# Projection phases of a two-layer decoder: another order at their start, weights of k converted ahead of tile 0, the norm gain in the output weights

## The reference

```python
for l in range(DEPTH):
    mod = silu(c) @ ada_w[l] + ada_b[l]                 # 6 rows of 1024
    sh1, sc1, g1, sh2, sc2, g2 = split(mod, 6)
    h = x * (1 + sc1) + sh1
    y = mlstm_mixer(h) if l == 0 else dilated_mixer(h, k_sh, v_sh, w_q, w_o)
    x = layer_norm(ALPHA * x + (1 + g1) * y, ...)
    h = x * (1 + sc2) + sh2
    x = layer_norm(ALPHA * x + (1 + g2) * hier_moe(h), ...)
    if l == 0:
        kv = x @ b_w_kv                                 # k and v, 3 * 8 * 64 columns each
        k_sh, v_sh = rope(kv[k]), kv[v]

def mlstm_mixer(h):
    q, k, v, o_gate, gates = split(h @ w_in)
    ht = mlstm_chunkwise(q, k, v, gates)                # (heads, tokens, 256)
    hn = (ht - mean) * rsqrt(var + 1e-6) * norm_g       # norm_g: 1024 gains
    return (hn * sigmoid(o_gate)) @ w_out
```

## Time and profile before

| | us |
|---|---|
| runs before, median of 3 | 4450.17 (4449.74 to 4456.16) |
| the profiled execution | 4457.96 |
| its span in the trace | 4456.2 |
| PE busy | 3855.9 (87% of the span) |
| DVE busy | 2224.4 (50%) |
| ACT busy | 1409.7 (32%) |
| POOL busy | 536.3 (12%) |

### The profile page before, as it was taken

How to read it: one execution, slowest core, us unless ns; L and a number is a source line. 1 busy time by engine, 2 the same in 40 slices (tenths; PEclk the granted TensorE clock), 3 DMA queues, 4 the chain that set the end, 5 groups by cost and what they waited for, 6 DMA issues and landing times. The chain is left out here.

```text
span 4456.2 us, 54326 instructions
## 1 busy us (share of the span) xinstructions
PE 3855.9 (87%) x17420; PEld 2852.8 (64%) x17420; DVE 2224.4 (50%) x4969; ACT 1409.7 (32%) x2977; POOL 536.3 (12%) x469
## 2 busy tenths in 40 slices
PE   6999794979949999995996998989996949999990
PEld 4777574868735565554885776868885736556550
DVE  3222314865455555556763333225436845555557
ACT  2212202632213333332222113216565413333334
POOL 0100000110001111104540002321000001111103
PEclk8999896979959999997998998999997959999995
DMA  6433312643239999986645433225454339999988
GB/s 232 142 119 122 124 66 98 194 141 105 74 120 391 389 388 391 389 317 202 191 147 182 170 138 110 77 73 174 120 161 167 128 108 384 389 391 389 389 330 316
DMA packets 662249, 951.11 MB, mean 213 GB/s; under 512 B 42317, under 2 KB 532765, under 8 KB 640845
## 3 DMA queue, kind: packets, MB, share of 16 engines
q1 hardware_dynamic: 607118, 772.87, 50.6%
q0 software_dynamic: 27360, 99.63, 5.8%
q10 hardware_dynamic: 27632, 76.87, 4.4%
HBM read 746.62 MB, written 202.65 MB: 213 GB/s over the span
## 5 line engine op out<-in xcount | busy, mean ns | idle before, releaser
L1517 PE MATMUL ex_gu<-ex_wgu,ex_hT 128*128 128x512 f32 x2016 | 911.2, 595 | 11.6 <-DMA ex_wgu<-in_moe_w_up_dram 8.0
L1517 PEld LDWEIGHTS ex_gu<-ex_wgu,ex_hT 128*128 128x128 f32 x2016 | 375.4, 191 | 388.3 <-issue 378.3
L1644 DVE TENSOR_TENSOR ex_wds<-ex_wd,ex_wds 128x2048 fp32r<-128x2048 f32 x126 | 288.8, 2292 | 247.2 <-ACT ex_wds L1577 247.2
L1535 PE MATMUL ex_acc<-ex_wds,ex_aT 128*128 128x512 f32 x1512 | 384.9, 404 | 7.7 <-DVE ex_aT L1640 7.7
L2199 PE MATMUL pvo_mm<-pvo_ws,pvo_hT 128*128 128x512 f32 x1536 | 360.7, 395 | 19.8 <-POOL pvo_hT L2348 18.4
L2199 PEld LDWEIGHTS pvo_mm<-pvo_ws,pvo_hT 128*128 128x128 f32 x1536 | 288.8, 190 | 83.4 <-POOL pvo_hT L2348 19.2
L1535 PEld LDWEIGHTS ex_acc<-ex_wds,ex_aT 128*128 128x128 f32 x1512 | 277.8, 190 | 65.1 <-DVE ex_aT L1640 8.1
L992 PE MATMUL am_acc<-am_ws,am_yT 128*128 128x512 f32 x1152 | 296.4, 413 | 19.7 <-issue 15.2
L1592 ACT ACTIVATE ex_sg<-ex_gu 128x256 f32<-128x256 f32 x126 | 48.4, 384 | 834.5 <-PE ex_gu L1517 834.5
L2199 PE MATMUL pk_mm<-pk_ws,pk_hT 128*128 128x512 f32 x1152 | 274.7, 397 | 28.4 <-DVE pk_part L2336 16.9
L2199 PE MATMUL pq_mm<-pq_ws,pq_hT 128*128 128x512 f32 x1152 | 268.4, 394 | 20.0 <-POOL pq_hT L2348 20.0
(11 more groups left out here) (337 smaller groups left out, 5655.0 us busy)
## 6 DMA issues: line engine op xcount, KB each, us to landing
ex_wgu<-in_moe_w_gate_dram SPq DMA_DIRECT2D x126, 1024.0 KB, 9.0
ex_wgu<-in_moe_w_up_dram SPq DMA_DIRECT2D x126, 1024.0 KB, 12.3
ex_wd<-in_moe_w_down_dram SPq DMA_DIRECT2D x126, 1024.0 KB, 6.5
ybuf_scratch<-ex_y ACTq DMA_DIRECT2D x126, 512.0 KB, 6.7
pv_m_w<-in_ada_w_dram SPq DMA_DIRECT2D x16, 1536.0 KB
pvo_r_w<-in_ada_w_dram SPq DMA_DIRECT2D x32, 512.0 KB
vo_scratch<-pvo_vo SPq DMA_DIRECT2D x16, 1024.0 KB, 5.0
x_scratch<-am_x SPq DMA_DIRECT2D x32, 512.0 KB, 3.0
```

The source lines that it names most:

```text
L1517: ins = nc.tensor.matmul(gu[j][:, :, :], hT[:, j, k, :], wgu[:, jw, k, :, :], start=(k == 0), stop=(k == KD - 1))
L1535: ins = nc.tensor.matmul(acc[half][:, :], aT[:, hi_a, k, :], wds[:, j, hi_w, k, half * CH:(half + 1) * CH], start=(k == 0 and n == 0), sto ...
L1644: nc.vector.tensor_tensor(wds[:, j, 1, :, :], wd[:, j, :, :], wds[:, j, 0, :, :], ALU.subtract).then_inc(wlo_ready, 1)
```

## The change

- **Projections, start.** SP first loads tile 0 (in k: `dest`, then tile 0's rows) and the identity and columns; the other tables follow, then tile 1 and the weights. ACT and DVE begin with the weight pieces and wait for the columns and constants only behind them. `FIRST` becomes 4 in vo, all 12 in k, 2 in v and q. The memset of v's value buffer and the start of the woven modulation move behind all weights.
- **k.** `dest` has a semaphore of its own, the only one that POOL's gather waits for. There is no `rest_of_weights`; tile 0's transposed copy and split run one step earlier (lead 2) than those of the other tiles.
- **vo.** The store of tile 0's `full` is put among the weight loads, behind piece 8. RestOfModulation's stages run one tile earlier, with two PSUM banks in place of one, and its store comes last in SP's list.
- **v.** LaterModulation's total runs one tile later, and DVE makes the partial before it adds the previous tile's bias.
- **mlstm and after_mixer of layer 0.** `ng` and `norm_gain` go; `gate` multiplies the normalised rows by the output gate directly. `MixerWeights` loads the gain as 128 x 8 (4 KB); ACT scales by it in `weights_hi`, DVE in `weights_lo`, each in two operations of 128 x 512 per piece in place of one of 128 x 1024.

```diff
@@ mlstm
-                sp.dma_start(ng[:, :], d["a_norm_g"][0:1, :].to_broadcast([P, D])).then_inc(c_in, 16)
...
                 def divide(c, j):
                     act.wait_ge(rden_ready, c + 1)
-                    wait_from(act, ng_done, c - 1)
+                    wait_from(act, y_ready, c - 1)
...
                 def gate(c, j):
                     dve.wait_ge(og_in[j], 8 * (c - j) + 16)
-                    dve.wait_ge(ng_done, c + 1)
-                    nc.vector.tensor_tensor(y[:, j, :], y[:, j, :], og[:, j, :], ALU.mult).then_inc(y_ready, 1)
+                    wait_from(dve, stored[j], 8 * (c - j))
+                    dve.wait_ge(hn_ready, c + 1)
+                    nc.vector.tensor_tensor(y[:, j, :], ht[:, j, :, :].rearrange("p h e -> p (h e)"), og[:, j, :], ALU.mult).then_inc(y_ready, 1)
...
-                def norm_gain(c, j):
-                    pool.wait_ge(hn_ready, c + 1)
-                    wait_from(pool, stored[j], 8 * (c - j))
-                    nc.gpsimd.tensor_tensor(y[:, j, :], ht[:, j, :, :].rearrange("p h e -> p (h e)"), ng[:, :], ALU.mult).then_inc(ng_done, 1)
-
-                skewed(pool, [(norm_gain, -1)])
@@ MixerWeights.load
         sp.dma_start(self.gain[:, :], d["mod"][self.l:self.l + 1, 2 * D:3 * D].to_broadcast([P, D])).then_inc(self.gain_in, 16)
+        if self.l == 0:
+            sp.dma_start(self.ng[:, :], d["a_norm_g"][0].rearrange("(p k) -> p k", k=self.K)).then_inc(self.ng_in, 16)
@@ after_mixer, weights_hi and weights_lo
-                        nc.scalar.activation(ws[:, 0, rows, cut], w[:, rows, cut], ACT.Copy).then_inc(whi_ready, 1)
+                            nc.scalar.activation(ws[:, 0, rows.start, cut], w[:, rows.start, cut], ACT.Copy, scale=mw.ng[:, rows.start:rows.start + 1])
+                            rows = slice(rows.start + 1, rows.stop)
+                        nc.scalar.activation(ws[:, 0, rows, cut], w[:, rows, cut], ACT.Copy, scale=1.0 if l else mw.ng[:, rows]).then_inc(whi_ready, 1)
...
-                        v.tensor_tensor(ws[:, 1, rows, cut], w[:, rows, cut], ws[:, 0, rows, cut], ALU.subtract).then_inc(wlo_ready, 1)
+                            for k in range(rows.start, rows.stop):
+                                ins = v.scalar_tensor_tensor(ws[:, 1, k, cut], w[:, k, cut], mw.ng[:, k:k + 1], ws[:, 0, k, cut], ALU.mult, ALU.subtract)
+                            ins.then_inc(wlo_ready, 1)
@@ RestOfModulation
-        self.acc = ph.ps("r_acc", [P, CW])
+        self.acc = [ph.ps(f"r_acc{s}", [P, CW]) for s in range(2)]
-        return [(load, 0), (store, -1)]
+        return [(load, 1), (store, 0)]
...
-                wait_from(pe, self.row_ready, n)
-                self.nc.tensor.matmul(self.acc[0:1, :], self.ones[:, :], self.part[:, s, :], start=True, stop=True).then_inc(self.acc_ready, 1)
-        return [(total, -1)]
+                wait_from(pe, self.row_ready, n - 1)
+                self.nc.tensor.matmul(self.acc[s][0:1, :], self.ones[:, :], self.part[:, s, :], start=True, stop=True).then_inc(self.acc_ready, 1)
+        return [(total, 0)]
...
-        return [(add_bias, -1), (partial, 0)]
+        return [(add_bias, 0), (partial, 1)]
@@ LaterModulation
-        return [(total, 0)]
+        return [(total, -1)]
-        return [(add_bias, -1), (partial, 0)]
+        return [(partial, 0), (add_bias, -1)]
@@ Combine
+    def sync_dest(self, sp):
+        sp.dma_start(self.dest[:, :, :].rearrange("p c j -> p (c j)"), self.d["dest"]).then_inc(self.dest_in, 16)
@@ project
-        FIRST = KD // WK
+        FIRST = {"vo": KD // WK, "k": KD // WK * NBK, "v": 2, "q": 2}[which]
...
+        def first_tile(stage):
+            return lambda c, j: stage(c, j) if isinstance(c, int) and c == 0 else None
+        def later_tiles(stage):
+            return lambda c, j: None if isinstance(c, int) and c == 0 else stage(c, j)
@@ project, sync
+                if fused:
+                    cb.sync_dest(sp)
+                    cb_load, cb_lead = cb.sync_stages(sp)[0]
+                    cb_load(0, 0)
+                else:
+                    first_load(0, 0)
+                sp.dma_start(ident[:, :], d["consts"][:, C_ID:C_ID + P]).then_inc(c_in, 16)
+                if modulated:
+                    load_mod_columns(sp, nc, d, cols, 0 if first_layer else 1, (0, 1), c_in)
...
+                        if first_layer and n == 2 * NPF:
+                            store_rows(0, 0)
...
+                consts()
                 if fused:
-                    for c in range(2):
-                        cb_load, cb_lead = cb.sync_stages(sp)[0]
-                        cb_load(c, c)
+                    cb_load(1, 1)
                     weights()
...
                 if lm:
-                    stages += lm.sync_stages(sp)
-                skewed(sp, stages + ([(store_rows, 1)] if first_layer or fused else []) + [(store_roped, -1) if roped_out else (store, 0)])
+                    stages += lm.sync_stages(sp)[:1]
+                if first_layer:
+                    stages += [(lambda c, j: None if isinstance(c, int) and c == 0 else store_rows(c, j), 1)]
+                skewed(sp, stages + ([(store_rows, 1)] if fused else []) + [(store_roped, -1) if roped_out else (store, 0)] + (lm.sync_stages(sp)[1:] if lm else []))
@@ project, scalar
+                weights_hi(range(FIRST))
                 if modulated:
                     act.wait_ge(cols_ready, 1)
-                if which == "v":
-                    act.wait_ge(ones_ready, 1)
-                if lm:
-                    lm.scalar_start(act)
-                weights_hi(range(FIRST))
...
+                if fused:
+                    skewed(act, [(later_tiles(transposed), 1), (later_tiles(whole_rows), 1), (first_tile(transposed), 2), (first_tile(whole_rows), 2)]
+                           + cb.scalar_stages(act) + [(turned, -1)])
@@ project, vector
-                if which == "v":
-                    v.memset(vo[:, :, :, :], 1.0).then_inc(ones_ready, 1)
...
                 weights_lo(range(FIRST))
+                dve.wait_ge(c_in, 16 * NC_IN)
+                if modulated:
+                    v.tensor_scalar(cols[:, 1, :], cols[:, 1, :], 1.0, None, ALU.add)
+                    dve.drain().then_inc(cols_ready, 1)
+                if fused:
+                    cb.vector_start(dve)
...
-                stages = combining[:1] + [(split, 1), (rest_of_weights, 1)] if fused else [(split, 1), (rest_of_weights, 1)]
+                stages = combining[:1] + [(first_tile(split), 2), (later_tiles(split), 1)] if fused else [(split, 1), (rest_of_weights, 1)]
@@ project, gpsimd
-                    pool.wait_ge(cb.cb_in, 48)
+                    pool.wait_ge(cb.dest_in, 16)
```

70 lines of the change are left out of this document (37 added, 33 removed).

## The result

The changed kernel takes **4417.59 us** (median of 4 runs, 4415.16 to 4421.27) against 4453.16 (4 runs, 4449.74 to 4457.73) beside it: ratio 0.992, 95% interval 0.9903 to 0.9937, or 35.6 us less. The forecast was 60.5 less, 4390, and its range ended at 4416, 1.6 us short. The sign was right and the gain too large. The profiled executions lie further apart than the medians: 4415.16 against 4457.96, 42.8 us. All that follows by phase is of these two.

The account below looks back on a forecast made before the run. PE, busy 87% of the span, bounds the kernel, so time is gained where it idles. Terms +2.7, -9, -5, -12, +0.5, -18, -17, -2.7 sum to -60.5: 4457.96 becomes 4397.5, less 7.8 gives 4390 us; range 4366 to 4416.

Parts of the forecast that it names:

- The steps: vo's step ends: two PSUM banks remove the 0.46 us wait and the trip around it at 14 ends, -9 us.
- the end: End of vo: the last small sums are done a tile earlier, so the next phase begins sooner, -5 us (-3 to -6).
- The start: Start of vo: ACT's 12.66 us wait goes, but earlier partial sums hold tile 1 until 88.2, +2.7 us.
- Rival 1: vo's new wait doesn't come because two modulation pieces land early; whole change -74 to -75, some 4376 us; chance 0.13.
- the ring: mLSTM's cycle of DVE, ACT and PE: without POOL 0.53 us shorter, period 10.84, -7.5 of the phase's -12 us.
- The case for k: k: by the contention rule two low halves beside POOL's sums each lose 2 us, T0 2038, k -16 instead of -18.
- Rival 3: mLSTM is bound by PE: mLSTM only -4.5, in all -53, some 4397 us; chance 0.20 together with rival 2.
- T0: k: end of the last low half, before tile 0 is combined; forecast at 2036 (2029 to 2045), bound by 9 MB of loads.
- Rival 2: k converts too late, gathers sharing DMA engines, T0 at 2045: -48 to -51, some 4400 us; chance 0.20 together with rival 3.
- Rival 4: DVE is held in every tile of v; slower from 3.8 us per step, 4.5 gives +11.5, 4462 us; chance 0.03.
- q, wrong sign: Start of q: only two pieces stand ahead of tile 0, forecast -2.7 us (-0.5 to -4).
- Mixer output: Mixer output: the gain goes into the output weights in two operations per piece, forecast +0.5 us (0 to +1.5).

Follow-up runs that it names:

- kernel 1: Changed kernel with vo's modulation stages on their old tiles, k's gathers held until all twelve pieces are converted, four pieces first in v and q: 4402.99 us.
- kernel 8: Changed kernel with vo's old leads and old store place; k stores before loads, no drain, rotation sums first; v's memset on POOL; four pieces in q: 4393.69 us.
- kernel 6: Changed kernel plus idle POOL product of two tiles in mLSTM, k stores first without drain, vo old leads with mid-tile totals, v and q edits: 4396.47 us.
- kernel 2: Changed kernel plus an idle POOL product of one tile with itself in mLSTM, output weights converted in whole pieces, four pieces first in q: 4411.27 us.
- kernel 3: Changed kernel with SP's stores ahead of its loads in k, vo's first modulation pieces loaded after piece 12, v's memset on POOL: 4404.04 us.
- kernel 10: Changed kernel with vo's old leads; k four pieces first, early tile 0 store, stores before loads, no drain, sums first; v's memset on POOL; q four: 4376.49 us.

## Why the prediction was right in part

**vo, right, but its start was a cancellation.** The steps were forecast at -9 and the end at -5; from the rows above they are 13 x (24.28 - 23.49) = -10.3 and 5.87 - 11.30 = -5.4. The start was forecast at +2.7 and tile 1 comes 3.3 later in its phase. Kernels 1 and 8 take that term apart. The early store is worth -14.0, all of it at the start. The earlier partials cost 17.9 there (15.5 of start and 2.4 of first bank) and give 4.5 back at the end, +13.4 in the phase. The forecast had both halves (12.66 us that go, an order of loads that brings PE to 88.2) and I did not draw the consequence that one half was best left out. Rival 1, the stall gone, put vo at 26 less than before; kernel 1, which takes the partials back, gives 425.48 - 399.46 = 26.0. Its mechanism did not occur by itself: the pieces landed where SP's order put them.

**mLSTM, right in the ring, short at the end.** The period is the forecast's, and kernel 6 shows the reason: DVE's operation is held to the end of POOL's instruction. The trace of before had it at 0.701, kernel 6 at 0.617. The prediction read this from a sentence on VectorE instructions with two SBUF inputs, and the operation has one. The Trainium skill (SBUF — State Buffer, Who interferes with whom) also lets a `tensor_scalar` contend with GpSimd where it runs in a mode that uses both ports, and there the one that comes second is blocked for the whole instruction. The hold to POOL's end agrees with that; which mode the operation ran in, no run shows. The case for k, of low halves held beside POOL's sums, turned on 2 us; the longest of the twelve took 2.22 here, and the term missed by 14 for other reasons. By steps: 12 of the 15 are 0.49 shorter each, -5.9; the second is 2.5 longer, PE's granted clock being 0.79 there and 0.88 before; the last full one is 6.65 shorter, the one after it 0.6; the phase's start is 1.5 shorter and its end 3.2. That makes -15.4. Rival 3 is out. The large term is one that I had not, and it takes the phase out of its range of -5 to -14: the last full step runs at clock 1.00 and not 0.56. Without that step and the second it is -11.3, near the forecast's -12. The clock falls ahead of that step in the two kernels with a period of 11.3 and in none of the eleven with 10.86 (kernel 2 among them, whose POOL works 1.89 us a step). Why it falls when it does stays open: no kernel tries the period apart from POOL's work.

**k, the step that failed: "-18 us (-6 to -27)", measured -4.1, outside its range.** Two parts of it:
- *T0, the rate.* It was worked out as 9 MB at 0.38 MB/us with the last piece at 2033.7, 26.9 into the phase, and low halves right behind it. T0 came 5.0 later, the last piece at +31.0. The bytes were right: 9.00 MB passed from the phase's start to T0, but at 263 GB/s in the mean, not 380. From 1988.94 to 1999.94 they ran at 371, in the 3 us after it at 174: the ring has four places, and SP could issue its second four pieces only from 2000.21 on, as DVE freed them. In kernel 1, without the gathers, the last piece lands at +25.7 (6.91 MB, 247 GB/s) and the last low half ends at +28.0. So, in one run each, the gathers cost the pieces 5.3 us, which is what the sum had for their 2 MB (2/0.38); the term was too small because it took 0.38 MB/us all the way, through the pause of the ring too. Rival 2 had T0 9 us late where 5.0 came, and its reason, the gathers, doesn't explain these 5.0. The page that it names, of the Trainium skill (DMA: Bandwidth & Descriptors, Queues, rings and completion order) has the queues served in turn; the trace agrees in so far as pieces come slower beside gathers, and shows no turn.
- *From tile 1 on.* I held tile 1 to run without a stall, and PE waits 2.05 ahead of it and 2.27 and 3.89 behind its first bank. The sum had nothing for them. Tile 1 starts at +66.2 where +59.2 was forecast, and -18 + 5.0 + 8.2 is -4.8, where -4.1 was measured. The first two go with SP's order (kernel 3), since store, weights and rows stand in one queue; the third, for POOL's drain that lets go only when a later tile's gather has landed, grows to 6.15 then, goes to 2.74 without the drain (kernel 6), and is gone with the sums first in POOL's list (kernel 8), at 355.94. In the three kernels with the changed k it took 365.4 to 367.9, so its gain is 1.6 to 4.1.

With all of it mended the term is 369.45 - 355.94 = -13.5 with all pieces first, and -19.0 with four (kernel 10). The forecast size was there to be had, not by this order.

**v, right mechanism, 3 us short.** Tile 0 is at +6.6 (+6.3 forecast). "Tile 1 follows tile 0 at once" failed: the memset was taken off the way of tile 0 and costed at nothing; it stands in the way of tile 1's values. Kernel 3 gives -19.8 with it on POOL (290.31), more than the forecast. Rival 4, DVE held in every tile, did not come: v is faster in all kernels.

**q, wrong sign.** I counted the pieces that stand ahead of tile 0, 1.2 of gain in the profile, and not when the ring of raw pieces is free to be refilled: with two pieces converted early, eight issues of SP take 20.98 us instead of 12.62 before, and tile 1 waits. The last of the eight is issued at +24.0 in its phase, before it was +20.0, and in kernel 1, with four pieces, +17.9. The kernels with four pieces took 309.8 to 311.8, -2.1 to -4.1 against before: the forecast's number with the old count. Those with two took 316.2 to 317.7.

**Mixer output, 2.2 for 0.5.** The row of 0.42 for 128x128 gave a fixed part of 0.3 and, for four pieces, 1.2 at most; 128x512 costs ACT 0.71, and eight took 5.02 and not 3.90, 1.1 more and within that bound. But ACT also began them 1.2 later in its phase (+5.26 against +4.04), for which the sum had nothing, and the first bank came 2.3 later (+13.3 against +11.1). In the other kernels with halves ACT began at +4.3 to +4.9, so part of the 2.2 is scatter.

**The last 7 us.** The forecast took the profiled execution of before to be 7.8 above its median. The changed kernel's profiled one is 2.4 below its own, and the runs of each kernel lie up to 8 us apart. Nothing in the two traces is needed for it.

## What to carry to other kernels

- When a forecast term is the sum of a large gain and a large cost at one place, write both as parts of the change that can be undone singly. Here one lead undone was worth more than a third of the whole change.
- Prefetch lists have two ends: what stands ahead of the first tile, and when the ring's places come free for the next loads. A store that others wait for belongs among the loads, at the place where its data are ready, not behind them.
- After a stall is taken away, follow the next tile through every engine to its end, with what each queue still has in flight then: three waits of 2 to 4 us stood behind a stall of 17.

## What the runs showed of the hardware

- POOL's drain behind two plain sums let go only when POOL's gather in flight had landed: sums ended at 2062.3, PE was let go at 2065.59 and POOL's next operation, which waits for the gather, began at 2065.66 (kernel 3: 2054.03, 2055.83, 2055.91). One step later, with no gather left in flight, POOL's next operation began 0.5 us behind the sums (2079.80, 2080.31). With the increment on the sum itself PE went on before the gather had landed (kernel 6).
- A DVE operation of 128x4 that takes 0.170 us takes 0.617 when a POOL product of two tiles runs, and ends with it (857.68 and 857.65). The product of one tile with itself is shorter on POOL, 1.89 us against 2.36; DVE's operation met only its last 0.13 us and stayed at 0.170.
- A period of 11.3 us in place of 10.86 went with more than itself: behind it the last full step of mLSTM ran at a granted clock of 0.56, behind the shorter at 1.00, which was 6.65 us in one step. The cause stays open.
- The tile that follows a long stall pays in its first bank too: 24 matmuls took 8.14 us after the waits in vo (granted clock 0.68), 8.63 in kernel 8 (0.64), and 5.74 in kernel 1 (1.00), where PE had stood for 0.68 us.
- Nine MB for the first 34 us of k passed at 263 GB/s in the mean and 371 in the best stretch. The rate fell to 174 between two rounds of a ring with four places.
